# Three buffers for the attention probabilities, and one more step between a score and its use

## The chip, the cores and the metric

One core of a Trainium2 chip. The metric is the time of one execution on the device, in microseconds (us). Each kernel is run several times; a number without a further word is the median. The core has five engines that run side by side and meet at semaphores: TensorE (PE in the profile; its weight loads are PEld), VectorE (DVE), ScalarE (ACT), GpSimd (POOL) and SyncE (SP, which here only issues transfers).

## The reference

One decoder layer for 512 tokens of width 1024, in float32:

```
h      = rms_norm(x, norm1_g) * (1 + scale1) + shift1          # six modulation rows: silu(c) @ w_ada + b_ada
proj   = h @ w_in  ->  q, k, v, qi, ki, wi, u_pool, g_attn, g_pool
q, k   = rms_norm over 64 channels of each of 8 heads
sel    = top 128 keys of each query, by the indexer's score (4 heads, relu, weighted sum, causal)
s      = q.k / 8 - slope(head) * distance      on the selected keys
attn   = softmax(s) @ v
merged = sigmoid(g_attn) * (attn @ w_attn_br) + sigmoid(g_pool) * (pooled(u_pool) @ w_pool_br)
x      = x + gate1 * (merged @ w_out)
h2     = rms_norm(x, norm2_g) * (1 + scale2) + shift2
up     = h2 @ w_up;  y = causal depthwise conv of width 3;  a, b = halves of y
out    = x + gate2 * ((silu(a) * b) @ w_down)
```

## The kernel before, in words

Activations are kept transposed (channels on the 128 partitions, 512 tokens along the row). Every float32 operand of a large product is split into a high part (rounded by ScalarE) and a low part (the rest, by GpSimd for weights and VectorE for activations), and three products are added: high with high, high with low, low with high. A weight chunk is loaded by SyncE into one of three `stage` slots, split by ScalarE (line 700, `high_parts`) and GpSimd (line 589, `low_parts`) into one of three `wsplit` slots, and multiplied by `high_products` (line 1374) and `low_products` (line 1383). `Schedule` and `schedule()` fix the order of all chunks; each has a bank of PSUM that must be drained by ScalarE or VectorE before it is used again.

The change lies in the attention stage, a loop over slots `t` that is written out on TensorE, ScalarE and VectorE. There are 32 steps (`STEPS`): 8 heads by 4 blocks of 128 queries. `step_of(t)` gives head and block: two heads alternate, and their blocks come in the order 0, 3, 1, 2, so steps 0 to 7 have 128, 128, 512, 512, 256, 256, 384, 384 keys, and this repeats every eight steps. Between the small products of the attention TensorE works on half a filler chunk in each slot (`filler(t)`): the high products in even slots, the low ones in odd slots. The 18 fillers are gp2, gp3 (slots 0 to 3), pb0, pb1 (4 to 7), gp4, gp5 (8 to 11), pb2, pb3 (12 to 15), gp6, gp7 (16 to 19), pb4 to pb7 (20 to 27), ga0 to ga3 (28 to 35). Those called pb have half as many products as the others (8 and 4 in place of 16 and 8).

What each engine does in slot `t` of the kernel before, in this order:

- TensorE: in even slots the scores of steps t and t+1 (line 1596); the transposes of the probabilities of step t-2 (line 1608) into `PT`; the filler half; the weighted sum of step t-3 (line 1629) out of `pT` into `HEADS`.
- ScalarE: where a head is finished, its high part out of `HEADS` (line 889); the ALiBi term of step t+1 (line 868); the exponential of step t into `prob` (line 899); the high part of the transposed probabilities of step t-2 into `pT` (line 907); every second slot the splitting of a weight chunk (line 700) and a gate's tanh (lines 826 and 882).
- VectorE: adds scores and ALiBi term and takes the row's maximum, `smax` (line 1254); the bias of the exponential (line 1258); for step t-1 the reciprocal of the sum and the normalisation of `prob` (lines 1263 and 1265); the low part of `pT` of step t-2 (line 1116); the low part of a finished head (line 1116 too, the rows with `qT`); with the pb fillers a product into `ypool` (line 1281).
- GpSimd: low parts of the filler weights (line 589), and after every fourth filler two rows of one modulation vector, as products and adds over 1024 columns (lines 644 to 648), whose input SyncE loads through the same `stage` slots.

`prob`, `logit`, `pT` and `PT` have two buffers each. The exponential of step t waits until the transposes of step t-2 are done (`prob_t`), and the scores of steps t and t+1 until the logits of step t-1 are (`logit_ok`). The weighted sum of a step waits for the low part of its probabilities (`pt_lo`). After the loop TensorE forms the modulation columns (line 1464), and then the attention's branch product, which waits for the last head (`head_lo`).

Of the kernel before, what the change touches and what calls it, by code (L numbers as in the profile page):

```python
# [5 lines left out]
F32 = mybir.dt.float32  # L6
F32R = mybir.dt.float32r
ALU = mybir.AluOpType
ACT = mybir.ActivationFunctionType
AX_X = mybir.AxisListType.X  # L10

P = 128
# [6 lines left out]
NT = S // P  # L19
# [34 lines left out]

NPAIRS = offset(NT)
STEPS = NT * H
SLOTS = STEPS + 4
ORDER = (0, 3, 1, 2)

FILLERS = tuple((kind, m + n) for kind, m in (("gp", 2), ("pb", 0), ("gp", 4), ("pb", 2), ("gp", 6), ("pb", 4),  # L60
# [10 lines left out]
def step_of(t):  # L71

    pair, r = divmod(t, 2 * NT)
    return 2 * pair + r % 2, ORDER[r // 2]


def finished(t):

    pair, e = divmod(t - 2 * NT - 2, 2 * NT)
    return (pair, e) if pair >= 0 and e < 2 else None  # L80


# [113 lines left out]
def build_layer(nc, x, c, w_ada, b_ada, norm1_g, w_in, q_norm_g, k_norm_g, w_attn_br, w_pool_grp, pool_scale,  # L196
# [19 lines left out]
    with ExitStack() as ctx:  # L216
# [43 lines left out]
        def arena(name, shape, dt, kb):  # L260
            return place(name, shape, dt, base + int(kb * K1))
# [36 lines left out]

        pT = arena("pT", [P, 2, 2, S], F32R, 80)
        logit = arena("logit", [P, 2, S], F32, 93)  # L300
        prob = arena("prob", [P, 2, S], F32, 97)

        macc = arena("macc", [P, D], F32, 103)
        nrm = arena("nrm", [P, 2, S], F32, 97)
# [380 lines left out]
        def _(act):  # L685
# [198 lines left out]

            for t in range(SLOTS):
                if finished(t) is not None:
                    m, e = finished(t)
                    act.wait_ge(pv_ok, t - 3)
                    me.did(act.activation(qT[e * HD:(e + 1) * HD, 0, m, :], HEADS[e][0:HD, :], ACT.Copy), head_hi)
                if t < STEPS:  # L890
                    if t + 1 < STEPS:
                        alibi_terms(t + 1)
                    h, i = step_of(t)
                    n = (i + 1) * P
                    act.wait_ge(bias_ok, t + 1)
                    if t >= 2:
                        act.wait_ge(prob_t, t - 1)
                    r = i * 2 * H + h
                    me.did(act.activation(prob[:, t % 2, 0:n], logit[:, t % 2, 0:n], ACT.Exp,  # L899
                                          bias=sbias[:, t:t + 1], scale=stat[:, 2, r:r + 1],  # L900
                                          accum_out=ssum[:, t:t + 1]), exp_ok)
                if 2 <= t < STEPS + 2:
                    n = (step_of(t - 2)[1] + 1) * P
                    act.wait_ge(prob_t, t - 1)
                    if t >= 4:
                        act.wait_ge(pv_ok, t - 3)
                    me.did(act.activation(pT[:, t % 2, 0, 0:n], PT[t % 2][:, 0:n], ACT.Copy), pt_hi)  # L907
                if t and filler(t - 1)[1] == "low":
                    kind, m = filler(t - 1)[0]
                    if kind == "gp":  # L910
                        pool_gate(m)
                    if kind == "ga":
                        gate(m)
                    if kind == "pb":
                        chunk((kind, m))
            gate(3)

            def load_mid(n):

                j, q = divmod(n, KD // 2)  # L920
# [80 lines left out]
        def _(dve):  # L1001
# [113 lines left out]
            def low_of(out_ap, full, hi, signal):  # L1115
                me.did(dve.tensor_tensor(out_ap, full, hi.bitcast(F32), ALU.subtract), signal)  # L1116
# [130 lines left out]

            for t in range(SLOTS):
                if t < STEPS:
                    h, i = step_of(t)  # L1250
                    n = (i + 1) * P
                    dve.wait_ge(linear, t + 1)
                    dve.wait_ge(score, t + 1)
                    me.did(dve.tensor_tensor_reduce(logit[:, t % 2, 0:n], logit[:, t % 2, 0:n], SC[t % 2][:, 0:n],
                                                    1.0, TAKEN, ALU.add, ALU.max, smax[:, t:t + 1]), logit_ok)
                    me.settle()
                    r = i * 2 * H + h
                    me.did(dve.tensor_scalar(sbias[:, t:t + 1], smax[:, t:t + 1], stat[:, 2, r:r + 1], -1.0,  # L1258
                                             ALU.mult, ALU.mult), bias_ok)
                if 1 <= t < STEPS + 1:  # L1260
                    n = (step_of(t - 1)[1] + 1) * P
                    dve.wait_ge(exp_ok, t)
                    me.did(dve.reciprocal(sinv[:, t - 1:t], ssum[:, t - 1:t]))
                    me.settle()
                    me.did(dve.tensor_scalar(prob[:, (t - 1) % 2, 0:n], prob[:, (t - 1) % 2, 0:n],  # L1265
                                             sinv[:, t - 1:t], None, ALU.mult), prob_ok)
                if 2 <= t < STEPS + 2:
                    n = (step_of(t - 2)[1] + 1) * P
                    dve.wait_ge(pt_hi, t - 1)
                    low_of(pT[:, t % 2, 1, 0:n], PT[t % 2][:, 0:n], pT[:, t % 2, 0, 0:n], pt_lo)  # L1270
                if finished(t) is not None:
                    m, e = finished(t)
                    r = slice(e * HD, (e + 1) * HD)
                    dve.wait_ge(head_hi, 2 * m + e + 1)
                    low_of(qT[r, 1, m, :], HEADS[e][0:HD, :], qT[r, 0, m, :], head_lo)
                if t and filler(t - 1)[1] == "low" and filler(t - 1)[0][0] == "pb":
                    name = filler(t - 1)[0]
                    m = name[1]
                    await_chunk(dve, name)
                    dve.wait_ge(drained["act"], drained_count[sch.chunk["gp", m]][1])  # L1280
                    me.did(dve.scalar_tensor_tensor(out=ypool[:, m, :], in0=ypool[:, m, :], scalar=1.0,
                                                    in1=bank(name)[:, :], op0=ALU.add, op1=ALU.mult),
                           drained["dve"])
# [83 lines left out]
        def _(pe):  # L1367
# [212 lines left out]
            low_products(sch.unit["gp", 1], bank(("gp", 1)), hT)  # L1580


            for t in range(SLOTS):
                if t < STEPS and t % 2 == 0:

                    h, i = step_of(t)
                    if t % (2 * NT) == 0:
                        pe.wait_ge(k_lo, h // 2 + 1)
                    if t == 0:
                        pe.wait_ge(kn_ok, 2)  # L1590
                    else:
                        pe.wait_ge(logit_ok, t)
                    for a, b in THREE:
                        for e in range(2):
                            r = slice(e * HD, (e + 1) * HD)
                            mm = pe.matmul(SC[e][:, 0:(i + 1) * P], qT[r, a, h // 2, i * P:(i + 1) * P],
                                           kT[r, b, h // 2, 0:(i + 1) * P], start=(a, b) == (0, 0), stop=a == 1)
                            if a == 1:
                                mm.then_inc(score, 1)
                if 2 <= t < STEPS + 2:  # L1600
                    i = step_of(t - 2)[1]
                    pe.wait_ge(prob_ok, t - 1)
                    if t < 4:
                        pe.wait_ge(kn_ok, t + 1)
                    else:
                        pe.wait_ge(pt_lo, t - 3)
                    for j in range(i + 1):
                        mm = pe.transpose(PT[t % 2][:, j * P:(j + 1) * P], prob[:, t % 2, j * P:(j + 1) * P],  # L1608
                                          ident[:, :])
                    mm.then_inc(prob_t, 1)  # L1610
                if filler(t):
                    name, part = filler(t)
                    if part == "high":
                        await_bank(pe, name)
                    (high_products if part == "high" else low_products)(
                        sch.unit[name], bank(name), mix if name[0] == "pb" else hT)
                if 3 <= t < STEPS + 3:
                    h, i = step_of(t - 3)
                    pe.wait_ge(pt_lo, t - 2)


                    if t - 3 == 1:
                        who, n = drained_count[max(k for k in range(sch.chunk[FILLERS[0]]) if sch.bank[k] == 2)]
                        pe.wait_ge(drained[who], n)
                    if (t - 3) % (2 * NT) < 2 and h >= 2:
                        pe.wait_ge(head_lo, h - 1)
                    for j in range(i + 1):
                        for a, b in THREE:
                            mm = pe.matmul(HEADS[h % 2][0:HD, i * P:(i + 1) * P], vS[:, j, a, h, :],  # L1629
                                           pT[:, (t - 1) % 2, b, j * P:(j + 1) * P],  # L1630
                                           start=j == 0 and (a, b) == (0, 0), stop=j == i and a == 1)
                    mm.then_inc(pv_ok, 1)
            mod_columns(2)
# [106 lines left out]
```

## Time and profile before

| | |
|---|---|
| median of 3 runs | 777.43 us (777.32 to 779.0) |
| the profiled execution | 777.76 us, its span 776.0 us |
| TensorE busy | 748.4 us (96%) |
| VectorE, ScalarE, GpSimd busy | 377.7, 308.2, 358.1 us |
| TensorE in the chain of work that ended last | 76% of the span |
| TensorE's granted clock | full speed (2.4 GHz) outside the first fortieths of the span |

The page has one row for each engine, a picture of the span in 40 slices, and the chain of work that ended last, followed back from the last instruction to what released each step. The other views go into a stretch: a table of busy time by stage, a list of waits (who waited for whom, in total, how often, and the longest), and a timeline with one line for a run of like instructions. In the timeline the columns are the start in us from the beginning of the span, the duration in us, engine, line, operation, output and inputs, the count, and in brackets the idle time of the engine before it with what ended it.

### The profile page before, as it was taken

What the parts mean: (1) busy time and instruction counts of PE and PEld (TensorE: products, weight loads), DVE (VectorE), ACT (ScalarE), POOL (GpSimd) and SP (SyncE); (2) the same over time, 40 slices, a digit from 0 to 9 for tenths busy, and PEclk for the clock granted to TensorE, in tenths of its full rate; (3) what the DMA queues carried; (4) which work ended last, traced back from release to release, by engine and by line L of the source; (5) the groups of instructions that cost most, each with busy time, mean ns of one, the idle gap of its engine ahead of it and who ended that gap; (6) DMA issues with size and microseconds to landing.
All of it is one profiled execution on the core that took longest, in us unless ns stands there. A gap on an engine that the chain in (4) does not pass through costs nothing.

```text
span 776.0 us, 9536 instructions
## 1 busy us (share of the span) xinstructions
PE 748.4 (96%) x3618; PEld 604.4 (78%) x3618; DVE 377.7 (49%) x682; ACT 308.2 (40%) x496; POOL 358.1 (46%) x187
## 2 busy tenths in 40 slices
PE   4889999999989999999999999999999999999998
PEld 2367788787777778888877888888888888888886
DVE  2562499954657872558937444545343433000000
ACT  4234423437655753333236344443344343222121
POOL 1125368346556583544943443444343444444250
PEclk9979999999999999999999999999999999999999
DMA  8933113231043343545755332233233321232401
GB/s 327 368 110 110 55 54 97 68 108 41 15 163 109 109 148 124 168 158 180 229 177 175 109 109 83 80 109 109 76 87 109 108 95 64 87 108 95 124 27 55
DMA packets 94461, 91.72 MB, mean 118 GB/s; under 512 B 2003, under 2 KB 85711, under 8 KB 94415
## 3 DMA queue, kind: packets, MB, share of 16 engines
q1 hardware_dynamic: 92239, 82.71, 33.5%
q10 hardware_dynamic: 2176, 8.39, 3.2%
q8 instruction: 29, 0.48, 0.2%
q14 instruction: 17, 0.14, 0.1%
HBM read 89.00 MB, written 2.10 MB: 117 GB/s over the span
## 4 chain that ended last, share of the span: by engine, by line
PE 76%; DVE 11%; issue 3%; DMA 3%; POOL 2%; ACT 2%; SPq 2%; ACTq 0%; DVEq 0%; POOLq 0%
PE bank L1374 45%; PE bank L1383 22%; DVE work L1158 2%; PE bank L1405 2%; DVE top L1155 2%; DMA ada<-in_w_ada_dram 2%; DVE macc L1047 2%; PE bank L1464 1%; PE bank L1410 1%; DVE prob L1265 1%; POOL wsplit L589 1%; PE bank L1629 1%; SPq L514 1%; DMA ada_mid<-in_w_ada_dram 1%; PE bank L1608 1%
## 5 line engine op out<-in xcount | busy, mean ns | idle before, releaser
L589 POOL TENSOR_TENSOR wsplit<-stage,wsplit 128x1024 fp32r<-128x1024 f32 (+2 forms) x127 | 288.8, 2279 | 370.9 <-ACT wsplit L700 370.9
L1374 PE MATMUL bank<-hT,wsplit 128*128 128x512 f32 x1200 | 286.9, 391 | 0.0
L1374 PEld LDWEIGHTS bank<-hT,wsplit 128*128 128x128 f32 x1200 | 223.9, 188 | 46.2
L700 ACT ACTIVATE wsplit<-stage 128x1024 fp32r<-128x1024 f32 (+2 forms) x127 | 125.5, 991 | 305.4 <-PE bank L1383 292.2
L1383 PE MATMUL bank<-hT,wsplit 128*128 128x512 f32 x600 | 150.0, 392 | 0.0
L1383 PEld LDWEIGHTS bank<-hT,wsplit 128*128 128x128 f32 x600 | 111.5, 188 | 23.8 <-issue 0.6
L1374 PE MATMUL bank<-guT,wsplit 128*128 128x512 f32 x352 | 84.0, 390 | 0.0
L1374 PEld LDWEIGHTS bank<-guT,wsplit 128*128 128x128 f32 x352 | 65.9, 188 | 13.5
L1336 DVE SCALAR_TENSOR_TENSOR yb<-bank,conv,yb 128x511 f32<-128x511 f32 (+1 forms) x44 | 33.0, 749 | 65.7 <-ACT yb L969 64.8
L1336 DVE SCALAR_TENSOR_TENSOR ya<-bank,conv,ya 128x511 f32<-128x511 f32 (+1 forms) x44 | 33.0, 750 | 60.4 <-ACT ya L969 59.7
L1361 DVE SCALAR_TENSOR_TENSOR xT<-bank,mod,xT 128x512 f32<-128x512 f32 x8 | 6.0, 751 | 111.5 <-PE bank L1383 111.5
L1383 PE MATMUL bank<-guT,wsplit 128*128 128x512 f32 x176 | 43.8, 389 | 0.0
L1383 PEld LDWEIGHTS bank<-guT,wsplit 128*128 128x128 f32 x176 | 33.0, 188 | 6.9
L1374 PE MATMUL bank<-merged,wsplit 128*128 128x512 f32 x128 | 32.9, 407 | 0.0
L899 ACT ACTIVATE prob<-logit,sbias,stat 128x128 f32<-128x128 f32 (+3 forms) x32 | 20.9, 652 | 30.1 <-DVE sbias L1258 23.1
L1374 PEld LDWEIGHTS bank<-merged,wsplit 128*128 128x128 f32 x128 | 24.9, 197 | 5.6 <-DVE msum L1299 0.2
L1047 DVE SCALAR_TENSOR_TENSOR macc<-ada_mid,csil,macc 128x1024 f32<-128x1024 f32 x14 | 28.4, 2031 | 0.5 <-DMA ada_mid<-in_w_ada_dram 0.2
L1265 DVE TENSOR_SCALAR prob<-prob,sinv 128x128 f32<-128x128 f32 (+3 forms) x32 | 27.9, 871 | 1.1
L1116 DVE TENSOR_TENSOR pT<-bank,pT 128x128 fp32r<-128x128 f32 (+3 forms) x32 | 15.6, 488 | 25.2 <-ACT pT L907 25.1
L1405 PE MATMUL bank<-hT,wsplit 128*128 128x512 f32 x64 | 21.8, 467 | 3.6 <-ACT hT L742 2.4
L1158 DVE MATCH_REPLACE8 work<-top,work 128x256 f32<-128x256 f32 (+2 forms) x45 | 24.0, 543 | 0.0
L1629 PEld LDWEIGHTS bank<-pT,vS 128*64 128x64 f32 x240 | 19.0, 135 | 4.8 <-DVE pT L1116 0.6
(182 smaller groups left out, 812.3 us busy)
## 6 DMA issues: line engine op xcount, KB each, us to landing
stage<-in_w_up_dram SPq DMA_DIRECT2D x44, 512.0 KB, 5.0
stage<-in_w_in_dram SPq DMA_DIRECT2D x17, 1024.0 KB, 5.1
ada_mid<-in_w_ada_dram ACTq DMA_DIRECT2D x8, 1024.0 KB, 5.8
stage<-in_w_down_dram SPq DMA_DIRECT2D x8, 1024.0 KB, 5.2
ada<-in_w_ada_dram SPq DMA_DIRECT2D x7, 1024.0 KB, 11.7
stage<-in_w_ada_dram SPq DMA_DIRECT2D x4, 1024.0 KB, 5.2
stage<-in_w_out_dram SPq DMA_DIRECT2D x4, 1024.0 KB, 7.1
ada_last<-in_w_ada_dram SPq DMA_DIRECT2D x4, 1024.0 KB, 8.5
```

Source lines behind the costliest of these rows:

```text
L589: pool.tensor_tensor(unit_split(n, 1), unit_source(n), unit_split(n, 0).bitcast(F32), ALU.subtract).then_inc(low, 1)
L700: me.did(act.activation(unit_split(n, 0), unit_source(n), ACT.Copy), high)
L899: me.did(act.activation(prob[:, t % 2, 0:n], logit[:, t % 2, 0:n], ACT.Exp, bias=sbias[:, t:t + 1], scale=stat[:, 2, r:r + 1], accum_out=s ...
L1047: me.did(dve.scalar_tensor_tensor(out=macc[:, :], in0=row, scalar=csil[:, k:k + 1], in1=macc[:, :], op0=ALU.mult, op1=ALU.add), mod_sum)
L1116: me.did(dve.tensor_tensor(out_ap, full, hi.bitcast(F32), ALU.subtract), signal)
L1158: me.did(dve.match_replace(out=row_of(work, i), in_to_replace=top8[:, i, :], in_values=row_of(src, i), imm_value=TAKEN))
L1265: me.did(dve.tensor_scalar(prob[:, (t - 1) % 2, 0:n], prob[:, (t - 1) % 2, 0:n], sinv[:, t - 1:t], None, ALU.mult), prob_ok)
L1336: me.did(dve.scalar_tensor_tensor(out=y[:, m % 2, back:], in0=bank((kind, m))[:, 0:S - back], scalar=w, in1=y[:, m % 2, back:], op0=ALU.mu ...
L1374: pe.matmul(out_bank[:, :], hi[:, k, :], rhs[:, part, k0 + k, :], start=first and k == 0 and part == 0, stop=False)
L1383: mm = pe.matmul(out_bank[:, :], lo[:, k, :], rhs[:, 0, k0 + k, :], start=False, stop=last and k == nk - 1)
L1405: pe.matmul(bank(name)[:, :], unit_split(sch.unit[name], 0)[:, k, :], hT[:, part, k, :], start=k == 0 and part == 0, stop=False)
L1629: mm = pe.matmul(HEADS[h % 2][0:HD, i * P:(i + 1) * P], vS[:, j, a, h, :], pT[:, (t - 1) % 2, b, j * P:(j + 1) * P], start=j == 0 and (a, ...
```

## The change

`prob` has three buffers. The transposes of a step stand three slots behind its scores in place of two, and the weighted sum four slots behind in place of three; the copy and the low part of the transposed probabilities, and the evacuation of a finished head, move by one slot with them. The exponential of step t waits for the transposes of step t-3. ScalarE's and VectorE's loops have one slot more, so the last gate falls into the loop. `logit`, `pT`, `PT`, the scores, the fillers and the normalisation keep their places, and no instruction is added or taken away.

```diff
-SLOTS = STEPS + 4
+SLOTS = STEPS + 5
 def finished(t):
-    pair, e = divmod(t - 2 * NT - 2, 2 * NT)
+    pair, e = divmod(t - 2 * NT - 3, 2 * NT)
-        prob = arena("prob", [P, 2, S], F32, 97)
+        prob = arena("prob", [P, 3, S], F32, 97)
...
                 if finished(t) is not None:
-                    act.wait_ge(pv_ok, t - 3)
+                    act.wait_ge(pv_ok, t - 4)
...
-                    if t >= 2:
-                        act.wait_ge(prob_t, t - 1)
+                    if t >= 3:
+                        act.wait_ge(prob_t, t - 2)
-                    me.did(act.activation(prob[:, t % 2, 0:n], logit[:, t % 2, 0:n], ACT.Exp,
+                    me.did(act.activation(prob[:, t % 3, 0:n], logit[:, t % 2, 0:n], ACT.Exp,
...
-                if 2 <= t < STEPS + 2:
-                    n = (step_of(t - 2)[1] + 1) * P
-                    act.wait_ge(prob_t, t - 1)
-                    if t >= 4:
-                        act.wait_ge(pv_ok, t - 3)
-                    me.did(act.activation(pT[:, t % 2, 0, 0:n], PT[t % 2][:, 0:n], ACT.Copy), pt_hi)
+                if 3 <= t < STEPS + 3:
+                    n = (step_of(t - 3)[1] + 1) * P
+                    act.wait_ge(prob_t, t - 2)
+                    if t >= 5:
+                        act.wait_ge(pv_ok, t - 4)
+                    me.did(act.activation(pT[:, (t - 3) % 2, 0, 0:n], PT[(t - 3) % 2][:, 0:n], ACT.Copy), pt_hi)
...
-            gate(3)
...
@@ VectorE
-                if 2 <= t < STEPS + 2:
-                    n = (step_of(t - 2)[1] + 1) * P
-                    dve.wait_ge(pt_hi, t - 1)
-                    low_of(pT[:, t % 2, 1, 0:n], PT[t % 2][:, 0:n], pT[:, t % 2, 0, 0:n], pt_lo)
+                if 3 <= t < STEPS + 3:
+                    n = (step_of(t - 3)[1] + 1) * P
+                    slot = (t - 3) % 2
+                    dve.wait_ge(pt_hi, t - 2)
+                    low_of(pT[:, slot, 1, 0:n], PT[slot][:, 0:n], pT[:, slot, 0, 0:n], pt_lo)
@@ TensorE
-            for t in range(SLOTS):
+            for t in range(SLOTS - 1):
...
-                if 2 <= t < STEPS + 2:
-                    i = step_of(t - 2)[1]
-                    pe.wait_ge(prob_ok, t - 1)
-                    if t < 4:
-                        pe.wait_ge(kn_ok, t + 1)
+                if 3 <= t < STEPS + 3:
+                    i = step_of(t - 3)[1]
+                    pe.wait_ge(prob_ok, t - 2)
+                    if t < 5:
+                        pe.wait_ge(kn_ok, t)
                     else:
-                        pe.wait_ge(pt_lo, t - 3)
+                        pe.wait_ge(pt_lo, t - 4)
...
-                if 3 <= t < STEPS + 3:
-                    h, i = step_of(t - 3)
-                    pe.wait_ge(pt_lo, t - 2)
+                if 4 <= t < STEPS + 4:
+                    h, i = step_of(t - 4)
+                    pe.wait_ge(pt_lo, t - 3)
...
-                    if (t - 3) % (2 * NT) < 2 and h >= 2:
+                    if (t - 4) % (2 * NT) < 2 and h >= 2:
                         pe.wait_ge(head_lo, h - 1)
```

## Rows read from the trace of the kernel before

**Rows 1.** List of waits, TensorE, 180 to 310 us: total, times, longest.

```profile
PE bank L1608 <- DVE prob L1265: 4.2, 6, 1.0
...
PE bank L1629 <- DVE pT L1116: 0.2, 1, 0.2
```

**Rows 2.** Busy time by stage: stretch, length, PE, PEld, DVE, ACT, POOL.

```profile
250.30:272.30 22.00, 20.45 (x154) 16.57 (x152) 18.16 (x50) 15.65 (x37) 12.51 (x7) 1.00 0.29 96
...
sum 121.00, PE 115.05 PEld 93.08 DVE 76.84 ACT 72.65 POOL 73.30; mean PE 23.01 PEld 18.61 DVE 15.37 ACT 14.53 POOL 14.66
```

**Rows 3.** Timeline of TensorE, slots 5, 6 and 8.

```profile
199.20 0.88 PE L1629 MATMUL bank<-pT,vS 128*64 128x128 f32 x12
200.01 0.79 PE L1596 MATMUL bank<-kT,qT 64*128 64x384 f32 x6
...
205.19 0.55 PE L1596 MATMUL bank<-kT,qT 64*128 64x128 f32 x6
206.63 0.55 PE L1608 MATMUL bank<-ident,prob 128*128 128x128 f32 x3 [0.88 <-DVE prob L1265]
```

**Rows 4.** Timeline of VectorE and GpSimd, VectorE's slots 6 and 7.

```profile
201.96 0.35 DVE L1265 TENSOR_SCALAR prob<-prob,sinv 128x256 f32<-128x256 f32 x1
...
203.99 2.37 POOL L589 TENSOR_TENSOR wsplit<-stage,wsplit 128x1024 fp32r<-128x1024 f32 x1 [1.97 <-ACT wsplit L700]
...
204.84 1.74 DVE L1265 TENSOR_SCALAR prob<-prob,sinv 128x384 f32<-128x384 f32 x1
```

**Rows 5.** Timeline, all engines, 216 to 229 us.

```profile
216.91 0.62 ACT L700 ACTIVATE wsplit<-stage 128x512 fp32r<-128x512 f32 x1
...
218.92 0.37 SPq L493 DMA_DIRECT2D stage<-in_w_ada_dram  x1
...
227.25 1.06 ACT L700 ACTIVATE wsplit<-stage 128x1024 fp32r<-128x1024 f32 x1 [2.88 <-issue]
...
228.21 0.58 ACT L826 ACTIVATE ypool<-bank 128x512 f32<-128x512 f32 x1
...
228.84 2.11 PE L1374 MATMUL bank<-mix,wsplit 128*128 128x512 f32 x8 [1.05 <-ACT ypool L826]
```

**Rows 6.** Timeline of TensorE, slots 15 and 16.

```profile
233.09 0.44 PE L1608 MATMUL bank<-ident,prob 128*128 128x128 f32 x2 [1.02 <-DVE prob L1265]
...
235.56 0.55 PE L1608 MATMUL bank<-ident,prob 128*128 128x128 f32 x3 [0.26 <-DVE prob L1265]
235.87 3.90 PE L1374 MATMUL bank<-hT,wsplit 128*128 128x512 f32 x16
```

**Rows 7.** Timeline of VectorE and GpSimd, VectorE's slots 20 to 27.

```profile
251.42 0.42 DVE L1254 CUSTOM_DVE_ANT_0 logit<-logit,bank 128x256 f32<-128x256 f32 x1
...
254.52 2.39 POOL L648 TENSOR_TENSOR macc<-macc,stage 128x1024 f32<-128x1024 f32 x1
...
254.73 2.33 DVE L1265 TENSOR_SCALAR prob<-prob,sinv 128x256 f32<-128x256 f32 x1
...
266.01 1.75 DVE L1265 TENSOR_SCALAR prob<-prob,sinv 128x128 f32<-128x128 f32 x1
...
271.62 0.67 DVE L1254 CUSTOM_DVE_ANT_0 logit<-logit,bank 128x512 f32<-128x512 f32 x1
```

**Rows 8.** Timeline of TensorE, slot 28.

```profile
272.36 0.62 PE L1596 MATMUL bank<-kT,qT 64*128 64x256 f32 x6 [0.56 <-DVE smax L1254]
273.92 0.66 PE L1608 MATMUL bank<-ident,prob 128*128 128x128 f32 x4 [0.94 <-DVE prob L1265]
274.34 3.92 PE L1374 MATMUL bank<-hT,wsplit 128*128 128x512 f32 x16
```

**Rows 9.** Timeline, TensorE and VectorE, the end of the loop.

```profile
300.00 0.70 PE L1629 MATMUL bank<-pT,vS 128*64 128x128 f32 x9
...
301.36 0.69 DVE L1116 TENSOR_TENSOR qT<-bank,qT 64x512 fp32r<-64x512 f32 x1 [3.56 <-ACT qT L889]
...
304.14 2.09 PE L1374 MATMUL bank<-qT,wsplit 128*128 128x512 f32 x8
```

More of the change, by code:

```diff
@@ L1264, in _ @@
                     me.settle()
-                    me.did(dve.tensor_scalar(prob[:, (t - 1) % 2, 0:n], prob[:, (t - 1) % 2, 0:n],
+                    me.did(dve.tensor_scalar(prob[:, (t - 1) % 3, 0:n], prob[:, (t - 1) % 3, 0:n],
                                              sinv[:, t - 1:t], None, ALU.mult), prob_ok)
-                if 2 <= t < STEPS + 2:
-                    n = (step_of(t - 2)[1] + 1) * P
-                    dve.wait_ge(pt_hi, t - 1)
-                    low_of(pT[:, t % 2, 1, 0:n], PT[t % 2][:, 0:n], pT[:, t % 2, 0, 0:n], pt_lo)
+                if 3 <= t < STEPS + 3:
[3 more added lines that the diff above has]
+                    low_of(pT[:, slot, 1, 0:n], PT[slot][:, 0:n], pT[:, slot, 0, 0:n], pt_lo)
                 if finished(t) is not None:
@@ L1599, in _ @@
                                 mm.then_inc(score, 1)
-                if 2 <= t < STEPS + 2:
-                    i = step_of(t - 2)[1]
-                    pe.wait_ge(prob_ok, t - 1)
-                    if t < 4:
-                        pe.wait_ge(kn_ok, t + 1)
+                if 3 <= t < STEPS + 3:
[3 more added lines that the diff above has]
+                        pe.wait_ge(kn_ok, t)
                     else:
-                        pe.wait_ge(pt_lo, t - 3)
+                        pe.wait_ge(pt_lo, t - 4)
                     for j in range(i + 1):
-                        mm = pe.transpose(PT[t % 2][:, j * P:(j + 1) * P], prob[:, t % 2, j * P:(j + 1) * P],
-                                          ident[:, :])
+                        mm = pe.transpose(PT[(t - 3) % 2][:, j * P:(j + 1) * P],
+                                          prob[:, (t - 3) % 3, j * P:(j + 1) * P], ident[:, :])
                     mm.then_inc(prob_t, 1)
@@ L1616, in _ @@
                         sch.unit[name], bank(name), mix if name[0] == "pb" else hT)
-                if 3 <= t < STEPS + 3:
-                    h, i = step_of(t - 3)
-                    pe.wait_ge(pt_lo, t - 2)
-                    if t - 3 == 1:
+                if 4 <= t < STEPS + 4:
+                    h, i = step_of(t - 4)
+                    pe.wait_ge(pt_lo, t - 3)
+                    if t - 4 == 1:
                         who, n = drained_count[max(k for k in range(sch.chunk[FILLERS[0]]) if sch.bank[k] == 2)]
                         pe.wait_ge(drained[who], n)
-                    if (t - 3) % (2 * NT) < 2 and h >= 2:
+                    if (t - 4) % (2 * NT) < 2 and h >= 2:
                         pe.wait_ge(head_lo, h - 1)
@@ L1629, in _ @@
                             mm = pe.matmul(HEADS[h % 2][0:HD, i * P:(i + 1) * P], vS[:, j, a, h, :],
-                                           pT[:, (t - 1) % 2, b, j * P:(j + 1) * P],
+                                           pT[:, t % 2, b, j * P:(j + 1) * P],
                                            start=j == 0 and (a, b) == (0, 0), stop=j == i and a == 1)
```

## The prediction, made before the changed kernel was run

> **What bounds the kernel now.** I read the page first: TensorE is busy 96% of the 776.0 us span and fills most of the chain that ended last, so only TensorE's idle time can be won, and only where the change acts. That is the head loop, 181.4 to 302.4 us. The table by stage over it gives 121.0 us, of which TensorE works 115.05; 5.95 us are idle [rows 2]. The list of waits names them: six waits of the transposes for the normalised probabilities, 4.2 us; one of the weighted sums for a low part, 0.2 [rows 1]. The rest are one wait of a filler for ScalarE's tanh, 1.05 [rows 5], and one of the scores for VectorE's logit (smax), 0.56 [rows 8]. By place the six are 0.88, 1.02, 0.26, 0.74, 0.31 and 0.94 us, 4.15 together. The reader is to see in the timeline why a normalisation is late: multiplying 256 columns takes 0.35 us, but 1.74 us for 384 columns while a POOL subtraction runs (203.99 to 206.36), and 2.33 us for 256 columns beside POOL's add of 254.52 [rows 4, 7].
>
> I count by slots t. TensorE now issues in slot t: scores of t and t+1 (even t), transposes of step t-2 (T), half a filler product, the weighted sum of step t-3 (PV). Scores 8 start at 205.19, scores 28 at 272.36 [rows 3, 8].
>
> **What is removed and added.** No instruction disappears. TensorE's order shifts T and PV by one step; slot 2 loses its transposes, slot 3 its sum, and T(31), PV(31) come one slot later. So the new kernel reaches every place of the loop "ahead" simply because one step is not done yet. This debt must be taken off before anything is called a gain. A PV of 12 products takes 0.81 us (199.20 to 200.01 [rows 3]), four transposes 0.42 (273.92 to 274.34 [rows 8]); so 0.07 and 0.1 each. The debt at the start of slot t is T(t-3) and PV(t-4): 0.6 us at slot 8 (2 transposes, 6 products), 1.2 at slot 14 (4 and 12), 0.7 at slot 19 (1 and 9), 0.3 at slot 28 (1 and 3).
>
> The exponential of t waits for the transposes of t-3 instead of t-2, but these stand in TensorE's slot t as their predecessors did: the third buffer frees ScalarE not a moment earlier. What it buys is distance: a normalisation made in VectorE's slot t+1 is now wanted in TensorE's slot t+3 and not t+2. ScalarE's copy and VectorE's low part of T are still wanted by the PV of the following slot, and scores still want the logit of t-1. Those two ties are untouched, and they are late next.
>
> **Slots 4 to 9.** The wait of 0.88 at T(6) goes, since the probabilities of step 5 were normalised at 202.3 [rows 4]. Next is the tie to the logit of step 7. VectorE's slot 6 gets the 512-wide low part of step 3 in place of a 256-wide one (about 0.3 us more), so I carry logit 7 to 205.1 us, where TensorE would arrive at 204.6 (205.19 less the debt): a wait of 0.5. T(6) follows a slot later behind a filler of 3.9 us (such as that of 235.87 [rows 6]). Gain 0.88 - 0.5, about 0.4; at the least 0, at the most 0.88. I carry 0.4.
>
> **Slots 10 to 16.** The idle 1.05 us at 228.84 comes from a load: ScalarE copies a weight at 216.91 once the exponential of step 10 is through, POOL subtracts, SyncE issues two transfers from 218.92, and ScalarE can split the second only at 227.25, after 2.88 us idle [rows 5]. SyncE's queue has the pool weight behind these two; ScalarE's has tanh, exponential 13 and a copy. The whole chain starts with scores 10 and moves forward with them, except for about 0.2 us, since the copy ahead of the weight is now 384 wide rather than 128. TensorE arrives earlier by its debt of 1.2 and waits correspondingly longer, about 1.6. Behind it ScalarE and VectorE are late as before, so the 1.02 and 0.26 at T(13), T(14) [rows 6] turn into waits of PV(10), PV(11) (512-wide copy and low part) and scores 16: I carry 0.3, 0.85 and 0.45. The following filler starts at 234.8 instead of 235.87: 1.07 ahead, 0.7 debt, net 0.4. So here nothing is won: of 1.28 us all is given back. Bounds for this stretch: 0.6 lost to 1.28 won; I take 0, nearest to the row of the load.
>
> **Slots 17 to 28.** The evacuation of a head pair, ScalarE's copy and VectorE's low part (0.69 us at 301.36 [rows 9]), moves from slots 18 and 19 to 19 and 20. VectorE's slot 19 hangs on TensorE's slots 18 and 19 and so comes earlier by the debt there, 0.65. From its logit 20 at 251.42 to logit 27 at 271.62, 20.2 us for seven slots, VectorE with ScalarE is a closed loop (logit, exponential, copy of T, low part, next logit) [rows 7]; the list of waits of this stretch names no TensorE for either. TensorE waits for it, being busy 20.45 of 22.00 us [rows 2]. The widths of the copies in these seven slots have the same sum before and after, and each has one head evacuation, so the loop keeps its length if the normalisations meet POOL as often. Two in it are lengthened: 2.33 (256 columns) and 1.75 (128). It starts 0.65 earlier plus the 0.4 of above. Hence scores 28 start at about 271.3 instead of 272.36: 1.05 ahead, 0.3 debt, net 0.8. And there the old kernel loses another 0.94 at T(26) [rows 8]; the new one has T(25) ready for long. That is the wait which truly goes, because long fillers (3.9 and 2.1 us) follow and VectorE is idle in them. Net 0.8 + 0.94, about 1.75. The waits of 0.74 and 0.31 inside the loop win nothing of their own: the loop sets the end.
>
> Bounds of the unknown phase between VectorE and POOL: a lengthened normalisation costs up to 1.98 (2.33 - 0.35) more, a spared one wins as much. TensorE's own work caps the win at the removed waits, 4.15 us.
>
> **The end of the loop.** PV(31) now stands behind the last low filler and starts at 301.85 instead of 300.00. From a PV's start to the end of its head's low part it is 2.05 us (300.00 to 301.36 + 0.69), so 303.9; the first product that needs the heads starts at 304.14 [rows 9], and the modulation columns cover the time between. If the cover went, up to 0.5 us. ScalarE's gate and the weight split start some 0.3 us later, behind the head's copy, and are wanted only after two products of the branch: nothing. The modulation transfers issued behind them by ScalarE's queue are later by as much: nothing.
>
> **Sum.** The profiled execution took 777.76 us (span 776.0 and 1.76 around it); less 1.75 is 776.0. It lay 0.33 above the median of the runs shown, 777.43, so against that I predict 775.7.
>
> **Two rules of the Trainium skill.** The trace shows a normalisation of 2.33 us beside a POOL add and 0.35 without [rows 4, 7]. The Trainium skill (SBUF — State Buffer, Who interferes with whom) says that a tensor_scalar in a two-port mode and a GpSimd instruction take the shared ports by an exclusive lock, the later one being fully blocked; the trace agrees. It speaks against this change: distance does not shorten a lock, and every shift deals the phases anew, which is the slower rival below. The six waits are all of one kind [rows 1]. The Trainium skill (Perfetto Trace Analysis, Optimization Strategy) says that consistent bubbles can mean too little SBUF for the next tile; by it more buffering would clear all of them, 773.3 instead of 775.7, which is the second rival; no run yet tells.
>
> **The rivals.**
> - The waits only move. Ties to logit and low part end as late as the normalisations did, everywhere; at most 0.5 us remains: 777.2. For it: slots 10 to 16 above, and the logit wait just before T(26). Against: after slot 28 there is no such tie.
> - All six waits go: 777.43 - 4.15 is 773.3. For it: they are equal in kind. Against: VectorE's loop from 251.42 to 271.62.
> - Slower. One place, VectorE's slots 20 to 27: POOL's adds and products of up to 2.4 us follow one another there, and the shifted normalisations begin just behind a POOL start twice more than now. Each costs 1.98: 3.96 - 1.75, 2.2 us later: 779.6. One more cancels the gain, the second decides. For it: POOL works over half of that time (12.51 of 22.00 [rows 2]). Against: two of seven are already hit, and a shift spares as easily.
> - The change does not do what it says: since the exponential's release is unmoved, the ScalarE side sets all ends, and the third buffer is empty gain: 777.4.
>
> **How the numbers follow.** Forecast 0.44 (own range 774.6 to 776.6), waits move 0.20, all go 0.15, slower 0.11, no effect 0.10. A measurement of this kernel tells about 0.2%, 1.55 us, from no change, so faster means below 775.9: of the forecast 0.31, and the 0.15, together 0.46; same 0.13 + 0.20 + 0.10, 0.43; slower 0.11. The range reaches to the second rival's time below and short of the slower one above, 773.5 to 778.0.
>
> **What would show it.** No wait of the transposes for the probabilities; instead waits of scores for the logit near slots 8, 16 and 28, and of sums for low parts near slot 15; a filler wait for tanh near 227.7 of some 1.6 us. Scores 28 near 271.3, the end of the loop near 300.7. VectorE from logit 20 to 27 again 20 us. It is wrong if that length changes by more than 1 us, if the transposes still wait, or if a gain inside the loop is gone behind it.

## The result, and the profile after

| | before | after |
|---|---|---|
| first comparison, medians | 777.58 us (4 runs) | 772.97 us (4 runs), ratio 0.9937 (95%: 0.992 to 0.9955) |
| second comparison | 777.1 us (15 runs) | 773.97 us (5 runs), ratio 0.9964 (0.9951 to 0.9976) |
| the profiled execution | 777.76 us, span 776.0 | 773.41 us, span 771.7 |
| TensorE idle between the first scores and the end of the head loop | 5.95 of 121.0 us | 3.57 of 118.85 us |

The changed kernel is faster, by 4.6 us in the first comparison and 3.1 in the second; 775.7 us was predicted, and 773.5 was the lower end of the range, so that the first comparison lies outside it and the second inside. Two more executions of the kernel before, of 942.29 and 2641.55 us, are disturbed and left out everywhere. The two profiled spans differ by 4.3 us. Three stretches hold it: 0.66 us ahead of the loop (the first scores start at 181.41 before and at 180.75 after), 2.16 us in it, and about 1.6 us behind it.

The list of waits of the changed kernel, TensorE, 180 to 310 us, answers to [rows 1]:

```profile
PE bank L1628 <- DVE pT L1114: 1.3, 4, 0.7
PE bank L1373 <- ACT ypool L826: 1.3, 1, 1.3
PE bank L1595 <- DVE smax L1252: 0.9, 3, 0.4
```

All six waits of the transposes for the normalised probabilities are gone, 4.2 us. In their place stand 1.1 us more for low parts, 0.3 more for the logit and 0.3 more for the tanh. The table by stage (same columns as [rows 2], the corresponding 22 us, then the sum over the loop) says the same: 1.17 us of idle time where there were 1.55.

```profile
248.30:270.30 22.00, 20.83 (x156) 16.48 (x154) 17.90 (x50) 15.67 (x36) 11.93 (x7) 1.00 0.29 96
...
sum 118.85, PE 115.28 PEld 92.71 DVE 75.82 ACT 72.22 POOL 73.21; mean PE 38.43 PEld 30.90 DVE 25.27 ACT 24.07 POOL 24.40
```

TensorE's timeline of the changed kernel, slots 8, 14 to 16, 28 and the end, against [rows 3, 5, 6, 8, 9]:

```profile
203.97 0.55 PE L1595 MATMUL bank<-kT,qT 64*128 64x128 f32 x6
204.45 0.44 PE L1607 MATMUL bank<-ident,prob 128*128 128x128 f32 x2
204.65 3.89 PE L1373 MATMUL bank<-hT,wsplit 128*128 128x512 f32 x16
...
226.58 2.11 PE L1373 MATMUL bank<-mix,wsplit 128*128 128x512 f32 x8 [1.33 <-ACT ypool L826]
228.88 0.94 PE L1628 MATMUL bank<-pT,vS 128*64 128x128 f32 x12 [0.19 <-DVE pT L1114]
...
231.64 0.94 PE L1628 MATMUL bank<-pT,vS 128*64 128x128 f32 x12 [0.66 <-DVE pT L1114]
232.80 0.55 PE L1595 MATMUL bank<-kT,qT 64*128 64x128 f32 x6 [0.23 <-DVE smax L1252]
...
233.47 3.88 PE L1373 MATMUL bank<-hT,wsplit 128*128 128x512 f32 x16
...
270.27 0.62 PE L1595 MATMUL bank<-kT,qT 64*128 64x256 f32 x6 [0.45 <-DVE smax L1252]
270.82 0.33 PE L1607 MATMUL bank<-ident,prob 128*128 128x128 f32 x1
270.90 3.92 PE L1373 MATMUL bank<-hT,wsplit 128*128 128x512 f32 x16
...
299.02 0.70 PE L1628 MATMUL bank<-pT,vS 128*64 128x128 f32 x9
...
301.32 2.11 PE L1373 MATMUL bank<-qT,wsplit 128*128 128x512 f32 x8
```

The reader is to see that the waits now stand at weighted sums and scores. VectorE's loop from logit 20 to logit 27 [rows 7] keeps its length, 20.46 us against 20.20:

```profile
249.06 0.42 DVE L1252 CUSTOM_DVE_ANT_0 logit<-logit,bank 128x256 f32<-128x256 f32 x1 [0.31 <-PE bank L1595]
...
269.52 0.68 DVE L1252 CUSTOM_DVE_ANT_0 logit<-logit,bank 128x512 f32<-128x512 f32 x1
```

**Behind the loop** there is a difference that the change does not touch in the code. First TensorE's timeline of the kernel before, then its table by stage (the third figure from the right is the granted clock, 1.00 for 2.4 GHz and 0.50 for 1.2 GHz); then the same of the changed kernel.

```profile
388.30 1.95 PE L1464 MATMUL bank<-ones,macc 128*128 128x1 f32 x16 [0.31 <-DVE macc L1047]
390.11 5.51 PE L1374 MATMUL bank<-merged,wsplit 128*128 128x512 f32 x16
```

```profile
388.00:392.00 4.00, 3.70 (x24) 3.34 (x25) 0.91 (x2) 3.06 (x4) 2.18 (x2) 0.95 0.50 127
392.00:396.00 4.00, 4.00 (x16) 3.23 (x14) 0.00 (x0) 0.00 (x0) 3.77 (x2) 0.62 0.02 4
```

```profile
385.52 1.95 PE L1463 MATMUL bank<-ones,macc 128*128 128x1 f32 x16 [0.34 <-DVE macc L1045]
387.32 3.92 PE L1373 MATMUL bank<-merged,wsplit 128*128 128x512 f32 x16
```

```profile
388.00:392.00 4.00, 4.00 (x24) 3.41 (x23) 0.00 (x0) 0.43 (x2) 4.00 (x3) 1.00 0.02 4
```

Sixteen wide products take 5.51 us in the one and 3.92 in the other: 1.59 us. Ahead of them TensorE did the same work in both: a wait of 0.3 us, and sixteen records of products with a single column (eight products in the code, each recorded twice).

Every run lists its mean granted clock, and half speed for some 3.4 us more is 0.002 of the span. Two things move it: this fall, and a slow stretch near 40 us, which by the tables by stage lasts 13.6 us in three of the profiles (a long start) and 10.2 in all others. The profiles here show a fall with a long start at 0.989 (the kernel before), a fall with a short start at 0.991 (experiment 1), a long start without a fall at 0.991 (experiment 4), and neither at 0.993 (the changed kernel). So 0.993 excludes both and 0.989 has both; 0.991 leaves it open which (0.992 belongs to a profile with neither, that of experiment 10). Of 52 runs of the kernel before that lie beside the kernels below, 1 had 0.993, 39 had 0.991 and 12 had less; of 9 runs of the changed kernel 7 had 0.993 and 2 had 0.989 (775.03 and 776.02 us). The times help where the mean clock does not: the one run of the kernel before at 0.993 took 774.38 us, the 39 at 0.991 took 776.22 to 777.65. So nearly all of them probably had the fall.

### The profile page after: what moved, and what is told of

It reads as the page before. It is cut to its first block, busy times and chain, and to the rows that moved or that the text cites. A ratio compares the mean times of both kernels' runs of the same rounds, so it can differ in the third digit from the quotient of the medians.

```text
span 771.7 us, 9535 instructions
## 1 busy us (share of the span) xinstructions
PE 747.6 (97%) x3618; PEld 603.4 (78%) x3618; DVE 377.5 (49%) x682; ACT 308.3 (40%) x496; POOL 357.6 (46%) x187
## 4 chain that ended last, share of the span: by engine, by line
PE 83%; DVE 9%; DMA 3%; SPq 2%; issue 1%; ACT 1%; ACTq 0%; DVEq 0%
PE bank L1373 48%; PE bank L1382 24%; DVE work L1156 2%; DVE top L1153 2%; PE bank L1404 2%; DMA ada<-in_w_ada_dram 2%; DVE macc L1045 2%; PE bank L1628 1%; PE bank L1607 1%; PE bank L1595 1%; PE bank L1463 1%; PE bank L1409 1%; SPq L514 1%; DMA ada_mid<-in_w_ada_dram 1%; PE bank L1518 1%
## 5 line engine op out<-in xcount | busy, mean ns | idle before, releaser
L1373 PEld LDWEIGHTS bank<-guT,wsplit 128*128 128x128 f32 x352 | 65.8, 188 | 13.6
L1373 PE MATMUL bank<-merged,wsplit 128*128 128x512 f32 x128 | 31.3, 392 | 0.0
```

The source lines that it names most:

```text
L1373: pe.matmul(out_bank[:, :], hi[:, k, :], rhs[:, part, k0 + k, :], start=first and k == 0 and part == 0, stop=False)
```

## The experiments

The loop's length below runs from the first scores to the first product of the attention branch in the profiled execution: 122.73 us before, 120.57 after.

**1. The third buffer alone.**

```diff
-        prob = arena("prob", [P, 2, S], F32, 97)
+        prob = arena("prob", [P, 3, S], F32, 97)
...
-                    if t >= 2:
-                        act.wait_ge(prob_t, t - 1)
+                    if t >= 3:
+                        act.wait_ge(prob_t, t - 2)
...
```

> The kernel before with three buffers for prob and nothing moved. Theory (distance between normalisation and transposes is what pays; the exponential is rarely held by its buffer): within 0.5 us of the kernel before, about 777.4, the six transposes' waits stay near 4 us. Rival (the buffer frees ScalarE): 2 us or more faster, the exponentials start earlier and the transposes' waits shrink.

777.02 us against 777.24, ratio 0.9997 (0.9988 to 1.0007); loop 122.71 us. The lists of waits of this kernel, TensorE, then ScalarE:

```profile
PE bank L1608 <- DVE prob L1265: 4.2, 6, 1.1
```

```profile
ACT prob L899 <- DVE sbias L1258: 26.6, 23, 2.8
```

In the kernel before the exponentials waited 6.8 us for transposes and 23.1 for the bias; now 26.6 for the bias and not at all for transposes. Most of ScalarE's wait only changed its name, the waits of the transposes stay at 4.2 us, and the buffer alone is worth nothing.

**2. The shift alone, with two buffers.**

```diff
-        prob = arena("prob", [P, 3, S], F32, 97)
+        prob = arena("prob", [P, 2, S], F32, 97)
...
-                    if t >= 3:
-                        act.wait_ge(prob_t, t - 2)
+                    if t >= 2:
+                        act.wait_ge(prob_t, t - 1)
...
```

> The changed kernel with two buffers for prob instead of three: transposes and weighted sums a step later, but each exponential must wait for the transposes of the slot after its own. Theory (the buffer is what makes the shift possible, it is no gain by itself): slower than the kernel before by 5 to 25 us, since scores, exponential and transposes then run one after the other between two slots. Rival (the shift alone carries the gain): 773 to 775 us.

794.13 us, ratio 1.0214 (1.0196 to 1.0232); loop 139.95 us. In its list of waits one row has grown from 2.5 us in the changed kernel (3 times; 6.8 us and 5 times in the kernel before):

```profile
ACT prob L899 <- PE bank L1607: 53.3, 29, 5.8
```

29 of 32 exponentials wait, 53.3 us in all, for transposes that TensorE issues in the slot after their own. (A part of the 17 us is the clock's, which is at 0.96 over the loop.) Buffer and shift are one edit: the first is worth nothing without the second, the second ruinous without the first.

**3. The changed kernel with everything behind the loop put back in time.**

```diff
             mod_columns(2)
+            keep_clock(12, hT[:, 0, 0, 0:P], hT[:, 0, 1, :])
             pe.wait_ge(head_lo, H)
```

> The changed kernel with 12 idle products (512 columns, 0.227 us each, 2.72 us in all) behind the head loop, so that everything after it stands in time where it stood in the kernel before. Theory A (of the 4.6 us about 1.6 came because TensorE's granted clock fell to half between 391.8 and 395.0 us of the kernel before and not in the changed one, and that hangs on when the thin products at 388.3 us come): the fall is back, 772.97 + 2.7 + 1.6 = 777.3 us. Rival B (the fall has its cause elsewhere, in what ran before it or in chance from run to run): 772.97 + 2.7 = 775.7 us, no fall or one as often as not.

777.8 us median of 10 runs, which fall apart: four with a mean clock of 0.993 (774.85 to 776.24), three with 0.991 and three with 0.989 (777.67 to 779.12 together). Its profiled execution is one of the last three:

```profile
388.21 1.95 PE L1463 MATMUL bank<-ones,macc 128*128 128x1 f32 x16 [0.34 <-DVE macc L1045]
390.01 5.49 PE L1373 MATMUL bank<-merged,wsplit 128*128 128x512 f32 x16
```

The fall is back at the place and with the length of the kernel before, behind the changed head loop, so the old loop is not what makes it; when the thin products come matters. But it is not back in all ten runs. The three at 0.989 surely have it; those at 0.991 took 777.93 to 778.11 us, about 2 us more than the mean of the four at 0.993 (775.88), and in experiment 9 the runs at 0.991 take only 0.2 us more than those at 0.993. By their times, then, six of ten had the fall. Theory A was too strict, a share of chance stays.

**4. Wide products around the thin ones, in the kernel before.**

```diff
+            keep_clock(2, qT[:, 0, 0, 0:P], qT[:, 0, 1, :])
             mod_columns(4)
+            keep_clock(2, qT[:, 0, 0, 0:P], qT[:, 0, 1, :])
```

> The kernel before with two idle products of 512 columns ahead of the thin modulation products at 388.3 us (they lie partly in the 0.31 us wait there) and two behind them, about 0.6 us of added work. Theory A (the thin, gappy stretch at 388 us makes the granted clock fall in the kernel before): no fall, 777.5 - 1.6 + 0.6 = 776.5 us. Rival B (the fall has nothing to do with that stretch): the fall stays, 778.1 us.

775.84 us, ratio 0.9985 (0.9976 to 0.9995), although work was added; the loop is unchanged, 122.73. The mean clock was 0.992 or 0.993 in eight of ten runs, and in the profile (0.991, with a long start) the wide products behind are at full speed:

```profile
387.83 1.95 PE L1464 MATMUL bank<-ones,macc 128*128 128x1 f32 x16
389.64 0.70 PE L1438 MATMUL bank<-qT 128*128 128x512 f32 x2
390.19 3.83 PE L1374 MATMUL bank<-merged,wsplit 128*128 128x512 f32 x16
```

That supports theory A: the thin stretch with its wait is what the clock answers to. The edit did not move that stretch, which begins 206.85 us behind the first scores (387.83 - 180.98) and began 206.89 us behind them before (388.30 - 181.41). The thin products behind the loop, which wait for nothing (1.84 us at 302.44 in the kernel before), have no fall behind them in any profile.

**5. The changed kernel again,** unedited.

> The changed kernel once more, in five rounds beside the kernel before, to see how often TensorE's granted clock falls behind 385 us. Theory A (where the thin products come decides): mean granted clock 0.993 in nearly every run, 772.5 to 773.5 us. Rival B (chance from run to run): the fall to half shows in about as many runs as in the kernel before, the median near 774.5 us.

773.97 us. Three runs at 0.993 (773.36 to 773.97), two at 0.989. Between the theories, nearer to A: with the first four runs 7 of 9 have no fall, while of the kernel before 12 of 52 surely have one and only 1 surely has none. The loop was 120.76 us. That the first four runs of the changed kernel all had 0.993 was in part luck, and a part of why the first comparison's gain is the larger one.

**6. ScalarE's weight copy ahead of the exponential** in slots 10 and 18 of the changed kernel.

```diff
+EARLY = (10, 18)
...
+                    if t in EARLY:
+                        pool_gate(filler(t - 1)[0][1])
                     if t + 1 < STEPS:
                         alibi_terms(t + 1)
...
-                if t and filler(t - 1)[1] == "low":
+                if t and t not in EARLY and filler(t - 1)[1] == "low":
```

> The changed kernel, ScalarE's weight copy and tanh of slots 10 and 18 put ahead of the exponential instead of behind it. In the changed kernel the copy stands at 214.6 us behind an exponential that begins at 213.4, while ScalarE was idle for 2.5 us, and the load that it releases makes a filler wait 1.33 us. Theory A (that chain sets the wait): the wait goes, and the waits of the sums and scores right behind it (0.66, 0.23) shrink, the head loop is 1.3 to 2.4 us shorter; 770.6 to 771.7 us if the clock does not fall, 1.6 more if it does. Rival B (the transfer is late for another reason): the filler still waits, no change in the head loop.

772.84 us, about 1 us below the changed kernel of the same comparison. In the loop theory A holds: 119.13 us, 1.4 less; the copy starts at 211.64 instead of 214.63, and no filler waits for tanh any more. The waits right behind did not shrink as expected: the sum's is 0.96 us in place of 0.66, the scores' is still 0.23. Behind the loop the mean clock was 0.991 in all five runs, 0.993 in none; in the profiled one it is a fall behind the thin products:

```profile
384.40 1.95 PE L1466 MATMUL bank<-ones,macc 128*128 128x1 f32 x16 [0.34 <-DVE macc L1048]
386.21 5.51 PE L1376 MATMUL bank<-merged,wsplit 128*128 128x512 f32 x16
```

The same products 1.1 us earlier than in the changed kernel, and in this execution the fall took 1.6 us, more than the loop had won. How many of the other four had it, their mean does not tell. Two runs took 773.86 and 773.9 us and three 772.27 to 772.84, so probably two of five had it, and not all five as experiment 11 supposes.

**7. and 8. Most of POOL's modulation work left out of the loop,** in both kernels: adds and products over 8 columns.

```diff
-                        pool.tensor_tensor(row, row, c_k, ALU.mult).then_inc(mod_term, 1)
+                        pool.tensor_tensor(row[:, 0:8], row[:, 0:8], c_k[:, 0:8], ALU.mult).then_inc(mod_term, 1)
...
-                        pool.tensor_tensor(macc[:, :], macc[:, :], row, ALU.add).then_inc(mod_sum, 1)
+                        pool.tensor_tensor(macc[:, 0:8], macc[:, 0:8], row[:, 0:8], ALU.add).then_inc(mod_sum, 1)
```

> The kernel before, leaving out most of one modulation vector: in the head loop POOL's products and adds (all but the first) run over 8 columns instead of 1024. Theory A (a good part of the transposes' waits is VectorE's normalisation held by POOL's work of about 2.4 us): the waits of the transposes fall from 4.2 to 1 to 2.5 us, the lengthened normalisations become few, the kernel is 2 to 3 us faster. Rival B (VectorE and ScalarE's own loop makes the waits): they stay near 4 us.

> The changed kernel with the same part left out (POOL's modulation work in the head loop over 8 columns instead of 1024). Theory A (the shift pays by covering normalisations held by POOL): the advantage of the shift in the head loop falls from 2.2 us to 0.5 to 1.5, against the kernel before with the same part left out. Rival B (it pays independently of POOL): the advantage stays 2 us or more.

777.56 us (1.0004, 0.9995 to 1.0013) and 773.97 us (0.9956, 0.9941 to 0.9972). Theory A fails in the first: the transposes still wait 3.9 us. Seven normalisations behind 197 us still take 1.2 to 2.35 us, each beside one of POOL's weight subtractions, as others were beside its adds before. And behind one of the waits the clock now fell in the loop itself (the kernel before with that part left out, TensorE and VectorE, then by stage):

```profile
234.19 1.71 DVE L1265 TENSOR_SCALAR prob<-prob,sinv 128x384 f32<-128x384 f32 x1
...
235.96 0.55 PE L1608 MATMUL bank<-ident,prob 128*128 128x128 f32 x3 [1.43 <-DVE prob L1265]
```

```profile
232.00:236.00 4.00, 2.03 (x19) 1.52 (x17) 3.59 (x8) 2.90 (x8) 2.35 (x1) 1.00 0.00 0
236.00:240.00 4.00, 4.00 (x13) 3.25 (x14) 3.07 (x13) 2.09 (x5) 1.28 (x1) 0.60 0.80 250
```

Its loop is 124.59 us, longer than with POOL's full work. With the shift it is 119.78. The advantage, 4.8 us, is not smaller; taking off the fall (1.6 us at 0.60 of the clock in 4 us) leaves 3.2. These are one profile each. So rival B: the shift pays without the modulation work too. It does not say how much it would pay without POOL's subtractions; that was not tried.

**9. and 10. The thin products dealt out between wide ones,** in both kernels; nothing is added.

```diff
-            mod_columns(4)
             final = ("wo", KD - 1)
             await_bank(pe, final)
-            high_products(sch.unit[final], bank(final), merged)
+            for k in range(KD + 1):
+                if k < KD:
+                    high_products(sch.unit[final], bank(final), merged, ks=range(k, k + 1))
+                if k == 1:
+                    pe.wait_ge(mod_sum, KD * 4)
+                    pe.wait_ge(mod_ok, 4)
+                if k:
+                    mm = pe.matmul(PT[0][:, MC + k - 1:MC + k], macc[:, (k - 1) * P:k * P], ones[:, 0:1],
+                                   start=True, stop=True)
+            mm.then_inc(mod_col, 1)
```

> The kernel before with the sixteen thin modulation products at 388.3 us dealt out between the 512-column products that follow them (two wide, one thin column, and so on), and their wait for VectorE behind the first two wide ones. Nothing is added. Theory A (thin products one after another, behind a wait, make the granted clock fall there): mean clock 0.993, no fall behind 385 us; 777.2 less 1.6 for the clock, less 0.3 to 0.6 for the wait: 775.0 to 775.4 us. Rival B (the fall is not bound to them): only the wait goes, 776.7 us, mean clock 0.991.

> The changed kernel with the same dealing out of the thin modulation products. Theory A: with the fall excluded in both, the changed kernel keeps only what the head loop gives, so it is 2.0 to 2.4 us faster than the kernel before with the same edit, and 0.4 to 0.8 faster than the changed kernel, mean clock 0.993 in nearly all runs: 772.3 to 773.2 us. Rival B (the whole 3 to 4 us comes from the loop and what follows it): 3.5 us or more between the two.

775.21 us, ratio 0.9974 (0.9965 to 0.9983), and 772.77 us, ratio 0.9944 (0.993 to 0.9958). Both times are as theory A had them, and neither profile has a fall behind 385 us. By stage, the kernel before with this edit:

```profile
388.00:392.00 4.00, 4.00 (x24) 3.50 (x23) 1.02 (x2) 3.06 (x4) 2.09 (x2) 1.00 0.52 141
392.00:396.00 4.00, 4.00 (x26) 3.52 (x25) 0.00 (x0) 0.00 (x0) 3.86 (x2) 1.00 0.02 4
```

The difference of the two is 2.4 us, and so is that of their loops (123.02 and 120.62 us). This is the change's own worth, freed of the clock. (The unshifted loop takes 122.71 to 123.02 us in the four profiles that leave its work as it is, the shifted one 120.57 to 120.76 in four.) The mean clocks, 0.991 to 0.993, are not all at the 0.993 that was expected; none is below 0.991, so no run had both a fall and a long start.

**11. Both additions.**

> Both additions on the changed kernel: ScalarE's early weight copy in slots 10 and 18, and the thin products dealt out. Theory A (the early copy gives 1.4 us in the head loop, hidden so far by a clock that fell in all five runs): mean clock 0.993, 770.8 to 771.6 us. Rival B (the earlier loop brings the fall somewhere else): 772.4 us and a mean clock of 0.991.

771.36 us, ratio 0.9927 (0.9914 to 0.9939), loop 119.19 us, no fall behind 385 us. It beats both kernels, 1.4 us below experiment 10. The gain of experiment 6 in the loop is now in the total.

## Why the prediction was wrong

**Right, with its size.** The head loop: 1.75 us were predicted, 2.16 measured in the first pair of profiles, 2.4 in experiments 9 and 10. The transposes no longer wait; the ties to logit and low part, which the prediction named as late next, cost 1.4 us more than before. VectorE's loop kept its length within 0.3 us of the forecast 20 us. Both the wait for tanh (1.33 against 1.6) and the evacuation at the end (no wait) came as said. The rival that the waits only move fails: 4.2 us went and 1.7 came. That all six go without any in their place fails as well. The slower rival fails in its own place: between logit 20 and logit 27 the same two normalisations are lengthened, 2.22 and 1.90 us against 2.33 and 1.75. The rival of no effect fails by the loop's 2.4 us.

**By stretch,** the ground gained less the debt, counted from the first scores:

| to the filler of slot | predicted | measured | how |
|---|---|---|---|
| 8 | 0.4 | 0.9 | 25.52 - 23.90, less 0.75 of debt |
| 16 | 0.4 | 1.0 | 54.46 - 52.72, less 0.7 |
| 28 | 1.75 | 2.2 | 92.93 - 90.15, less 0.6 |

The term mis-sized is the logit wait at slot 8. It was set at 0.5 us and did not come: VectorE's slot 6 began 0.6 us earlier than carried (logit 6 at 199.77 us, 200.43 on the clock of the profile before), because the slots ahead of it moved with the debt too. The prediction took VectorE as standing still there and moved only TensorE.

Two of its sums do not come out. From the filler at 227.7, about 5.8 us of work (6.89 less 1.08 of waits in the changed kernel) and the carried 0.3, 0.85 and 0.45 give 235.1 for the filler of slot 16 and not 234.8, a net 0.1 in place of 0.4; the three waits measured 0.19, 0.66 and 0.23. And the lower end of the range, 773.5, does not reach the second rival's 773.3.

**Wrong.** The step that failed is the sum, which puts every change outside the loop at nothing without a reason: "less 1.75 is 776.0". With it fails the bound beside it, "TensorE's own work caps the win at the removed waits, 4.15 us", which 4.6 us exceeds though the loop's idle time fell by only 2.38. What lies outside the loop did change: 1.6 us of the first comparison's 4.6 came because TensorE kept 2.4 GHz behind the thin products at 385.52 us where, behind those at 388.30, it had run at 1.2 GHz for about 3.4 us. Experiments 4 and 9 show the link to the thin products; in 3 the same code, shifted later, has the fall again in some of its runs, and in 6, shifted earlier, in its profiled run. The kernel before had the loss in plain sight in a row that was not read: 5.51 us for sixteen wide products that take 3.9 elsewhere. The table ahead of the prediction has TensorE at full speed outside the first fortieths of the span; it was read from the page's digits, where a slice of 19.4 us with this fall still shows a 9, while the stages of 4 us show 0.95 and 0.62. The Trainium skill (TensorE: Matmul & The Clock Gate, Part 1) says that the monitor behind the clock runs freely and does not start with the kernel; the mixed outcomes of experiments 3 and 5 agree. In the second comparison, where two of the five changed runs had the fall, the gain was 3.1 us and 773.97 lies in the range; that the sum left out the clock shows less there, and is wrong all the same.

The last 0.66 us lies ahead of the loop, where both kernels are alike. The first scores start between 180.10 and 181.41 us in the profiles of this case, all with the same code up to there, so it is within the spread between executions, and no effect of the change.

**Open:** why the profiles show the fall behind thin products at 384.40, 386.99, 388.21, 388.30 and (experiment 2) 405.10 us, and none behind those at 384.19, 385.52, 385.56 and 389.28. The start in the span alone does not decide it. The same kernel falls in one run and not in another. The experiments show that the stretch and probably its moment matter, not the rule by which they do.

## What to carry to other kernels

When a wait is met by pulling producer and consumer apart, buffer and order have to move together, and the debt of work not yet done must be taken off before a gain is read. Then look for what the shift moves far away: read the granted clock by stage and look for products that take longer than their like, behind every wait and every run of single-column products. Spread thin products between wide ones; here that added no work and took 777.36 to 775.21 us, and a small gain elsewhere is no longer eaten or doubled by the clock.

## What the runs showed of the hardware

Behind a wait of 0.3 us and 1.95 us of single-column products the granted clock fell to half for some 3.4 us in the profiles of five kernels. It did not in four profiles of three others, whose thin products and wait are the same and come at another moment. A normalisation over 256 or 384 columns, 0.35 or 0.42 us by itself, took up to 2.55 us (experiment 8, at 196.64 us) beside POOL's weight subtractions of about 2.4, so that removing POOL's modulation work did not remove the waits.
